# The MLP norm's weights: from per-partition factors after the turn to a row that is multiplied in with the token scale

## The chip, the cores and the metric

One Trainium2 chip, one of its cores. The time is device microseconds of one execution of the whole kernel; that of a kernel is the median of its runs. Engines are called as in the profile: PE (matrix products and transposes; PEld loads their weights), DVE (vector engine), ACT (scalar engine), POOL (here it issues DMAs), SP (issues most of the weight loads).

## The reference, cut to what matters

One layer of a decoder: 2048 prompt tokens and 64 sample tokens, 1024 channels, float32.

```
x = x + W_out [ RMSNorm(attention) || RMSNorm(o * h_mlstm) ]
x = x + channel_mlp(x, norm_mlp, w_up, w_down)

def rmsnorm(x, g):
    y = x * rsqrt(mean(x * x) + EPS)
    return y * g

def channel_mlp(x, g, w_up, w_down):
    h = rmsnorm(x, g)                    # g is norm_mlp, 1024 values
    u = maximum(h @ w_up, 0)
    return (u * u) @ w_down
```

## The kernel before

The tokens are worked off in four quarters of 512 (four tiles of 128; the last quarter has a fifth tile of 64 sample tokens). Each quarter goes through the input projection, attention and the mLSTM, the output projection, the norm that this change is about, and the MLP. Float32 products are made of two halves: each operand is split into a high part (rounded to fp32r by a Copy on ACT) and a low part (the difference, on DVE), and three matmuls are added. So the MLP's input is wanted as `a_hi` and `a_lo`, with channels on the partitions, and also whole in `x_all` (`x_flat`), since from the third unit on the up projection is done in seven products of half size, whose operands are sums of parts of `x_all` (`x_sums` on DVE, `t_high_part` on ACT, `t_low_part` on DVE).

Every engine's order of work is written out by hand; semaphores (`Signal`) tie them. Around the norm, in a quarter that is not the last:

- ACT: `square_tile` of tiles 0 and 1 (sum of squares L886, root L888), `high_tile(0)` (L897), the high part of the first half of the first up weights (`split_act`, L838), `high_tile(1)`, the second half, `square_tile` 2 and 3, `high_tile` 2 and 3, then the high parts of the next unit's weights, then the T parts of the sums and `plain_up` (L1243: Relu of the first up products).
- DVE: for each tile five short instructions for the token scale and `norm_tile` (L1518: x times the token scale, 128x1024); reads of the output projection (`op_at`); for each tile `take_tile` (the turned tile in PSUM times the weights, into `x_all`) and `low_tile` (`a_lo`); between them `split_vec` (L1417: low parts of the weights). Both `take_tile` and `low_tile` show as L1456, the helper for every tensor_tensor. The order is: norm 0, two reads, norm 1, take 0, low 0, read, weights, take 1, low 1, weights, two reads, norm 2, norm 3, take 2, low 2, take 3, low 3, two weights, `x_sums`.
- PE: `turn` (L2511: eight transposes of one tile into two PSUM banks of 4 to 7) of tiles 0 and 1 between the last products of the output projection (L2470 to L2472); then it waits for the low parts of the first up weights and of tiles 0 and 1, does the first up products on these two tiles, with `turn` of tiles 2 and 3 in between, waits for the low parts of all tiles (`nlow`), does the other half, the next up unit (L2470 to L2472), and then the seven products (L2987 to L2989). A bank of `turn` may be written again when `xf_ok` says that its `x_all` part is done.
- POOL: small DMAs. In each quarter it copies eight rows for the mLSTM (`lines`), and after the last product of the MLP's up projection loads the bias tables of the attention again (`bias_again`), since their memory, `bias`, is shared with the MLP's buffers. `sc_read` counts the attention's reads of the bias tables (L1890).

In the last quarter there are five tiles, in the order 0, 1, sample, 2, 3, and ACT does the square of the third tile between `high_tile(0)` and `high_tile(1)`, and both halves of the first up weights after `high_tile(1)`.

The weights `norm_mix`, `norm_attn_out`, `norm_mlstm_out` and `norm_mlp` are read at the start as 24 rows of 128 and turned once (`gains_turn`), so that each channel's weight is a value of its partition.

Of the kernel before, what the change touches and what calls it, by code (L numbers as in the profile page):

```python
# [6 lines left out]
F32 = mybir.dt.float32  # L7
F32R = mybir.dt.float32r
I32 = mybir.dt.int32
ALU = mybir.AluOpType  # L10
ACT = mybir.ActivationFunctionType
# [3 lines left out]
P = 128  # L15
D = 1024
KT = D // P
SEQ = 2048
DECB, DECT = 8, 8
NS = DECB * DECT  # L20
H, KVH, DH = 8, 2, 64
# [16 lines left out]
BLK = TQ // P  # L38
# [145 lines left out]
def norm_order(NT):  # L184

    return [0, 1, BLK, 2, 3] if NT > BLK else [0, 1, 2, 3]
# [22 lines left out]
def hymba_layer(nc, x_prompt, x_sample, cache_k_win, cache_v_win, state_C, state_n, state_m, rel_bias,  # L209
# [5 lines left out]
    with ctx:  # L215
        def sb(name, shape, dt=F32, where=ctx):
            return where.enter_context(nc.sbuf_tensor(name, shape, dt))
# [12 lines left out]
        a_hi = sb("a_hi", [P, KT, TMAX], F32R)  # L230
        a_lo = sb("a_lo", [P, KT, TMAX + NS], F32R)
        sample_parts, sample_again = slice(TQ, TMAX + NS), slice(TMAX, TMAX + NS)
        x1_forms = other("x1_forms", [P, BLK + 1, D], F32R)
        x1 = sb("x1", [P, BLK + 1, D])
        square = sb("square", [P, 4, P])
        ident, triu, ntriu, cmask = (square[:, i, :] for i in range(4))
        kwin = other("kwin", [P, P], F32)[:, 0:KVH * DH]
        ones = sb("ones", [P, P], F32R)
        gains = sb("gains", [P, 3, KT])
        g_final = sb("g_final", [P, D])  # L240
        nsink = sb("nsink", [P, H])
        sink = sb("sink", [P, H])
# [7 lines left out]
        PT = sb("PT", [P, 4, 4 * P])  # L250
        st = sb("st", [P, 240])
# [28 lines left out]
        bias = sb("bias", [P, H, 2 * P], where=phase)  # L280
# [39 lines left out]
        ps = [ctx.enter_context(nc.psum_tensor(f"ps{b}", [P, 512], F32)) for b in range(8)]  # L320
# [10 lines left out]
        early_vec = signal("early_vec", 0)  # L331
# [5 lines left out]
        xf_ok, t_sum, t_high, t_split = signal("xf_ok", 2 * BLK), signal("t_sum", 4), signal("t_high", 4), signal("t_split", 4)  # L337
# [10 lines left out]
        gains_in = signal("gains_in", 0)  # L348
# [5 lines left out]
        normed = signal("normed", BLK)  # L354
        turned = signal("turned", 2 * BLK)
# [3 lines left out]
        nhigh, nlow = signal("nhigh", 2 * BLK), signal("nlow", 2 * BLK)  # L359
# [16 lines left out]
        sc_out, sc_read = signal("sc_out", 2 * BLK), signal("sc_read", H * BLK)  # L376
# [25 lines left out]
        early_pe = signal("early_pe", 0)  # L402
# [2 lines left out]
        act = signal("act", PER_ACT)  # L405


        gain_rows = PT[0:3 * KT, 0, 0:P]
        bucket = bias[0:NBUCKET + 1, 0:2, :].rearrange("p a b -> p (a b)")[:, 0:3 * P]
        bias_by_distance = bias[0:H, 2:4, :].rearrange("p a b -> p (a b)")[:, 0:3 * P]  # L410
        rel_rows = bias[0:NBUCKET + 1, 4, 0:H]
# [6 lines left out]
        def xn_tile(j):  # L418
            return wide[:, 4 * (j % 2):4 * (j % 2) + 4, :].rearrange("p a b -> p (a b)")
# [103 lines left out]
        def x_flat(last):  # L523

            w = TMAX + NS if last else TMAX
            starts = (4 * w, 8 * w + (2 * TQ if last else 4 * TMAX))
            return [x_all[:, at:at + 4 * v].rearrange("p (k t) -> p k t", k=4) for at, v in zip(starts, (w, TMAX))]
# [27 lines left out]
        def spare():  # L555

            return t_plain[:, 0:D]

        def turned_bank(q, n):

            return n % 4
# [135 lines left out]

        @block.gpsimd
        def _(pool):
            for row, g in ((0, norm_mix), (8, norm_attn_out), (12, norm_mlstm_out), (16, norm_mlp)):  # L700
                src = g[0, :].rearrange("(k p) -> k p", p=P)
                pool.dma_start(gain_rows[row:row + src.shape[0], :], src).then_inc(gains_in.sem, 16)
            pool.wait_ge(x_in[3].sem, x_in[3].at(0, 16))
# [23 lines left out]
            def lines(q):  # L727

                if q:
                    pool.wait_ge(m_out.sem, m_out.at(q, 0))  # L730
                pool.wait_ge(r_rows.sem, r_rows.at(q, 2))
                for j in range(BLK):
                    for n, part in enumerate((Mhigh, Mlow)):
                        pool.dma_start(Mline[32 * j + n:32 * j + n + 1, :].rearrange("p (h t) -> p h t", h=HM), part[:, j, :]).then_inc(m_line.sem, 16)

            for q in range(QM):
                lines(q)
# [10 lines left out]
            with nc.allow_non_contiguous_dma("n, and short rows of the bias"):  # L748
                for h in range(H):
                    g, par = h // GQ, h % 2  # L750
# [62 lines left out]
        def _(eng):  # L813
# [76 lines left out]
            def high_tile(q, NT, k):  # L890

                n = norm_order(NT)[k]
                R = NS if n == BLK else P
                s = slice(n * P, n * P + R)
                for m in range(2):
                    eng.wait_ge(xf_ok.sem, xf_ok.at(q, 2 * k + m + 1))
                    eng.activation(a_hi[:, 4 * m:4 * m + 4, s], x_flat(NT > BLK)[m][:, :, s], ACT.Copy).then_inc(nhigh.sem, 1)  # L897

            def high_heads(q, j):

# [508 lines left out]
        def _(eng):  # L1409
# [45 lines left out]
            def tt(out, a, b, op):  # L1455
                return eng.tensor_tensor(out, a, b, op)  # L1456
# [54 lines left out]
            def norm_tile(q, NT, k):  # L1511

                n = norm_order(NT)[k]
                R = NS if n == BLK else P
                scale_tile(q, n, k + 1, root_count(NT > BLK, k))
                if k >= 2:
                    eng.wait_ge(turned.sem, turned.at(q, 2 * (k - 1)))
                eng.tensor_scalar(xn_tile(k)[0:R, :], x1[0:R, n, :], st[0:R, 132 + n:133 + n], None, ALU.mult).then_inc(normed.sem, 1)  # L1518

            def take_tile(q, NT, k):  # L1520

                n = norm_order(NT)[k]
                R = NS if n == BLK else P
                for m in range(2):
                    eng.wait_ge(turned.sem, turned.at(q, 2 * k + m + 1))
                    gain = gains[:, 2, 4 * m:4 * m + 4].unsqueeze(2).broadcast_to([P, 4, R])
                    tt(x_flat(NT > BLK)[m][:, :, n * P:n * P + R], ps[4 + (2 * k + m) % 4][:, 0:4 * R].rearrange("p (k t) -> p k t", k=4), gain, ALU.mult).then_inc(xf_ok.sem, 1)

            def low_tile(q, NT, k):

                n = norm_order(NT)[k]
                R = NS if n == BLK else P
                s = slice(n * P, n * P + R)
                for m in range(2):
                    eng.wait_ge(nhigh.sem, nhigh.at(q, 2 * k + m + 1))
                    tt(a_lo[:, 4 * m:4 * m + 4, s], x_flat(NT > BLK)[m][:, :, s], a_hi[:, 4 * m:4 * m + 4, s].bitcast(F32), ALU.subtract).then_inc(nlow.sem, 1)

            def final_norm(q):

# [451 lines left out]
            def quarter(q, last):  # L1991
# [220 lines left out]
                if last:  # L2212
                    op_at(3, BLK)
                    norm_tile(q, NT, 1)
                    take_tile(q, NT, 0)
                    low_tile(q, NT, 0)
                    op_at(2, 2)
                    norm_tile(q, NT, 2)
                    take_tile(q, NT, 1)
                    low_tile(q, NT, 1)  # L2220
                    op_at(2, 3)
                    split_vec(eng, q, U_M, 0)
                    op_at(3, 2)
                    split_vec(eng, q, U_M, 1)
                    take_tile(q, NT, 2)
                    low_tile(q, NT, 2)
                else:
                    op_at(2, 2)
                    norm_tile(q, NT, 1)
                    take_tile(q, NT, 0)  # L2230
                    low_tile(q, NT, 0)
                    op_at(2, 3)
                    split_vec(eng, q, U_M, 0)
                    take_tile(q, NT, 1)
                    low_tile(q, NT, 1)
                    split_vec(eng, q, U_M, 1)
                    op_at(3, 2)
                op_at(3, 3)
                norm_tile(q, NT, NT - 2)
                norm_tile(q, NT, NT - 1)  # L2240
                take_tile(q, NT, NT - 2)
                low_tile(q, NT, NT - 2)
                take_tile(q, NT, NT - 1)
                low_tile(q, NT, NT - 1)
                ws, c_at, s1, r6, h5, s5 = staging(last)

                def x_sums():

                    one, two = x_flat(last)
                    x11, x12, x21, x22 = one[:, :, HT:TQ], one[:, :, 0:HT], two[:, :, HT:TQ], two[:, :, 0:HT]  # L2250
                    eng.wait_ge(nlow.sem, nlow.at(q, 2 * NT))
                    tt(x11, x12, x11, ALU.subtract).then_inc(t_sum.sem, 1)
                    tt(x12, x22, x12, ALU.subtract).then_inc(t_sum.sem, 1)
                    eng.wait_ge(t_sum.sem, t_sum.at(q, 2))
                    tt(x22, x22, x11, ALU.subtract).then_inc(t_sum.sem, 1)
                    if last:
                        tt(two[:, :, TQ:TMAX], two[:, :, TQ:TMAX], one[:, :, TQ:TMAX], ALU.subtract)
                    eng.wait_ge(t_sum.sem, t_sum.at(q, 3))
                    tt(x21, x22, x21, ALU.subtract).then_inc(t_sum.sem, 1)
# [177 lines left out]
            root_ahead(0, 0)  # L2437
            first_scale(0)
            eng.wait_ge(early_pe.sem, early_pe.at(0, 1))
            eng.tensor_copy(gains[:, :, :].rearrange("p a k -> p (a k)"), ps[7][:, 0:3 * KT]).then_inc(early_vec.sem, 1)  # L2440
            split_vec(eng, 0, 0, 0)
            eng.wait_ge(early_vec.sem, early_vec.at(0, 1))
            for m in range(4):
# [17 lines left out]
        def _(eng):  # L2461
# [63 lines left out]

            def gains_turn():

                eng.wait_ge(gains_in.sem, gains_in.at(0, 16 * 4))
                eng.transpose(ps[7][:, 0:3 * KT], gain_rows, ident[0:3 * KT, 0:3 * KT]).then_inc(early_pe.sem, 1)

            def first_turn(b):

# [599 lines left out]
```

## Time and profile before

| | us |
|---|---|
| median of 3 runs | 2346.86 (2346.73 to 2352.06) |
| the profiled execution | 2347.0 |
| its span on the core | 2345.2 |
| PE busy in the span | 2300.8 |
| DVE, ACT, POOL busy | 1665.1, 1104.1, 94.6 |

The profiled execution's time is the span and 1.8 us around it. The granted clock of PE was 0.997 of full speed in the mean. The busy times of a matmul overlap with the next one's, so PE's idle time is read from the waits and the timeline.

### The profile page before, as it was taken

Reading aid. Unit: us, or ns where it says so; the run is one execution under the profiler, and the core shown is the slowest. Engines: PE = TensorE matmul, PEld = TensorE weight load, DVE = VectorE, ACT = ScalarE, POOL = GpSimd, SP = SyncE. Lnnn points to the kernel's source line nnn. Section 1 sums busy time; section 2 is a strip of 40 time slices with the busy share of each in tenths; the row PEclk is TensorE's granted clock in tenths of the full one; section 3 lists DMA queues with packets and bytes.
Section 4 is the critical chain, followed back from the end, with each engine's and each line's share of the span. In section 5 each row is a group of like instructions: output and inputs, shape, how many; then the busy total and the mean of one; then the engine's idle time right before and its main releaser. Section 6 shows DMA issues by size and latency. Waiting matters only on the chain.

```text
span 2345.2 us, 37363 instructions
## 1 busy us (share of the span) xinstructions
PE 2300.8 (98%) x14430; PEld 2040.1 (87%) x14430; DVE 1665.1 (71%) x3597; ACT 1104.1 (47%) x2110; POOL 94.6 (4%) x161
## 2 busy tenths in 40 slices
PE   9999999999999999999999999999999999999998
PEld 8987899888897898898998788999878878989986
DVE  4478877777368877777456887777755788776775
ACT  4445544445345644455333554444534545444433
POOL 3000000000000000000000220000110000000000
PEclk9999999999999999999999999999999999999999
DMA  6212333234511232334521232333444112222222
GB/s 196 81 46 80 99 99 102 96 100 152 167 56 54 73 100 95 103 99 144 159 81 37 62 94 96 108 99 101 160 123 135 43 53 82 91 90 82 90 81 77
DMA packets 176652, 227.93 MB, mean 97 GB/s; under 512 B 15507, under 2 KB 126708, under 8 KB 176460
## 3 DMA queue, kind: packets, MB, share of 16 engines
q1 hardware_dynamic: 162636, 192.63, 26.4%
q10 hardware_dynamic: 6448, 19.40, 2.3%
q0 software_dynamic: 7392, 13.52, 2.0%
q8 instruction: 115, 1.88, 0.3%
q14 instruction: 61, 0.50, 0.1%
HBM read 214.13 MB, written 12.60 MB: 97 GB/s over the span
## 4 chain that ended last, share of the span: by engine, by line
PE 88%; DVE 8%; ACT 2%; issue 1%; DVEq 0%; ACTq 0%
PE ps L2470 18%; PE ps L2472 18%; PE ps L2471 18%; PE ps L2987 8%; PE ps L2988 8%; PE ps L2989 8%; PE ps L2481 2%; PE ps L2615 2%; PE ps L2595 1%; DVE w_lo L1417 1%; DVE a_lo L1456 1%; PE ps L2604 1%; PE ps L2661 1%; PE ps L2664 1%; DVE x_all L1456 1%
## 5 line engine op out<-in xcount | busy, mean ns | idle before, releaser
L2470 PE MATMUL ps<-w_hi,u_all 128*128 128x512 f32 x1024 | 403.1, 394 | 1.4 <-DVE w_lo L1417 1.4
L2472 PE MATMUL ps<-w_hi,u_all 128*128 128x512 f32 x1024 | 404.2, 395 | 0.0
L2471 PE MATMUL ps<-w_lo,u_all 128*128 128x512 f32 x1024 | 400.2, 391 | 0.0
L1456 DVE TENSOR_TENSOR x<-x,ps 128x512 f32<-128x512 f32 (+1 forms) x288 | 196.3, 684 | 135.1 <-PE ps L2472 117.4
L866 ACT ACTIVATE w_hi<-PT 128x512 fp32r<-128x512 f32 x224 | 128.4, 621 | 340.4 <-PE ps L2472 237.1
L2470 PE MATMUL ps<-w_hi,a_hi 128*128 128x290 f32 (+1 forms) x768 | 262.0, 341 | 1.3 <-DVE x L1456 0.9
L2987 PE MATMUL ps<-a_hi,w_hi 128*128 128x256 f32 (+1 forms) x896 | 255.5, 285 | 1.4 <-DVE wide L1456 1.4
L2988 PE MATMUL ps<-a_lo,w_hi 128*128 128x256 f32 (+1 forms) x896 | 255.8, 285 | 0.0
L2989 PE MATMUL ps<-a_hi,w_lo 128*128 128x256 f32 (+1 forms) x896 | 255.2, 285 | 0.0
L2471 PE MATMUL ps<-w_lo,a_hi 128*128 128x290 f32 (+1 forms) x768 | 252.6, 329 | 0.0
L2472 PE MATMUL ps<-w_hi,a_lo 128*128 128x290 f32 (+1 forms) x768 | 252.4, 329 | 0.0
L2472 PEld LDWEIGHTS ps<-w_hi,u_all 128*128 128x128 f32 x1024 | 192.1, 188 | 44.3
L2471 PEld LDWEIGHTS ps<-w_lo,u_all 128*128 128x128 f32 x1024 | 192.4, 188 | 43.0
L2470 PEld LDWEIGHTS ps<-w_hi,u_all 128*128 128x128 f32 x1024 | 192.3, 188 | 43.0 <-DVE w_lo L1417 2.7
L1456 DVE TENSOR_TENSOR wide<-ps,wide 128x256 f32<-128x256 f32 (+2 forms) x350 | 140.0, 415 | 112.8 <-PE ps L2989 110.9
L1417 DVE TENSOR_TENSOR w_lo<-w_raw,w_hi 128x1024 fp32r<-128x1024 f32 (+1 forms) x160 | 176.5, 1114 | 52.8 <-ACT w_hi L838 52.8
L2470 PE MATMUL ps<-a_hi,w_hi 128*128 128x512 f32 (+2 forms) x552 | 188.7, 342 | 12.2 <-DVE a_lo L1456 8.0
L1223 ACT ACTIVATE wide<-wide 128x512 f32<-128x512 f32 (+1 forms) x112 | 72.3, 645 | 254.7 <-DVE wide L1456 254.7
L2472 PE MATMUL ps<-a_hi,w_lo 128*128 128x512 f32 (+2 forms) x552 | 187.2, 339 | 0.0
L2471 PE MATMUL ps<-a_lo,w_hi 128*128 128x512 f32 (+2 forms) x552 | 186.9, 339 | 0.0
L2987 PEld LDWEIGHTS ps<-a_hi,w_hi 128*128 128x128 f32 x896 | 169.1, 189 | 4.4 <-DVE wide L1456 2.0
L2988 PEld LDWEIGHTS ps<-a_lo,w_hi 128*128 128x128 f32 x896 | 169.1, 189 | 2.4
(427 smaller groups left out, 4904.8 us busy)
## 6 DMA issues: line engine op xcount, KB each, us to landing
w_raw<-in_w_up_dram SPq DMA_DIRECT2D x128, 512.0 KB, 4.0
w_raw<-in_w_down_dram SPq DMA_DIRECT2D x128, 512.0 KB, 3.5
w_raw<-in_w_out_dram SPq DMA_DIRECT2D x32, 512.0 KB, 3.5
w_raw<-in_w_in_dram SPq DMA_DIRECT2D x24, 580.0 KB, 4.7
w_raw<-in_w_in_dram SPq DMA_DIRECT2D x22, 512.0 KB, 3.8
w_raw<-in_w_in_dram SPq DMA_DIRECT2D x32, 256.0 KB, 3.0
x<-in_x_prompt_dram ACTq DMA_DIRECT2D x9, 512.0 KB, 5.9
bias<-bias_rows POOLq DMA_DIRECT2D x32, 128.0 KB, 3.5
```

The lines of the kernel that those rows point to most:

```text
L866: eng.activation(form_at(w_hi_all, u, f), form_src(q, u, name), ACT.Copy).then_inc(f_high.sem, 1)
L1223: eng.activation(c_at[phi], c_at[phi], ACT.Relu).then_inc(u_rel.sem, 1)
L1417: ins = eng.tensor_tensor(w_lo_all[:, to:to + b - a], src[:, a:b], w_hi_all[:, to:to + b - a].bitcast(F32), ALU.subtract)
L1456: return eng.tensor_tensor(out, a, b, op)
L2470: eng.matmul(out, lh, rh, start=(k == ks[0]), stop=False)
L2471: eng.matmul(out, lh, rl, start=False, stop=False)
L2472: ins = eng.matmul(out, ll, rh, start=False, stop=(k == last))
L2481: ins = eng.matmul(out, lhs(k), right, start=(k == ks[0] and part == 0), stop=(k == ks[-1] and part == 1))
L2615: ins = eng.matmul(values_at(g)[:, h, :], PT[:, 2 * g + half, h * P:(h + 1) * P], vv[:, j + half, g, :], start=(half == 0), stop=(half == 1))
L2987: eng.matmul(out, hi[:, k, :], rh, start=(k == 0), stop=False)
L2988: eng.matmul(out, hi[:, k, :], rl, start=False, stop=False)
L2989: ins = eng.matmul(out, lo[:, k, :], rh, start=False, stop=(k == 3))
```

## The change

The weights of the MLP norm are no longer turned: they are read, in each quarter, as one row of 1024 values copied to all 128 partitions (512 KB), by a DMA of POOL, into the first half of the bias tables' memory (`g_mlp`), once the quarter's last score has been read. `norm_tile` multiplies by the token scale and this row in one `scalar_tensor_tensor`. `take_tile` is gone. ACT makes `a_hi` straight from the turned tile in PSUM, DVE makes `a_lo` from the same PSUM bank, and ACT then copies the tile from PSUM to `x_all`, after the low part of that half tile is done. `x_sums` waits for these copies.

```diff
-        gains = sb("gains", [P, 3, KT])
+        gains = sb("gains", [P, 2, KT])
...
-        gain_rows = PT[0:3 * KT, 0, 0:P]
+        gain_rows = PT[0:2 * KT, 0, 0:P]
+        g_mlp = bias[:, 0:4, :].rearrange("p a b -> p (a b)")
...
+        def turned_tile(k, m, R):
+            return ps[4 + (2 * k + m) % 4][:, 0:4 * R].rearrange("p (k t) -> p k t", k=4)
...
-            for row, g in ((0, norm_mix), (8, norm_attn_out), (12, norm_mlstm_out), (16, norm_mlp)):
+            for row, g in ((0, norm_mix), (8, norm_attn_out), (12, norm_mlstm_out)):
...
                         pool.dma_start(Mline[...], part[:, j, :]).then_inc(m_line.sem, 16)
+                pool.wait_ge(sc_read.sem, sc_read.at(q, H * BLK))
+                pool.dma_start(g_mlp, norm_mlp[0, :].partition_broadcast(P)).then_inc(gains_in.sem, 16)
...
             def high_tile(q, NT, k):
                 for m in range(2):
-                    eng.wait_ge(xf_ok.sem, xf_ok.at(q, 2 * k + m + 1))
-                    eng.activation(a_hi[:, 4 * m:4 * m + 4, s], x_flat(NT > BLK)[m][:, :, s], ACT.Copy).then_inc(nhigh.sem, 1)
+                    eng.wait_ge(turned.sem, turned.at(q, 2 * k + m + 1))
+                    eng.activation(a_hi[:, 4 * m:4 * m + 4, s], turned_tile(k, m, R), ACT.Copy).then_inc(nhigh.sem, 1)
+                for m in range(2):
+                    eng.wait_ge(nlow.sem, nlow.at(q, 2 * k + m + 1))
+                    eng.activation(x_flat(NT > BLK)[m][:, :, s], turned_tile(k, m, R), ACT.Copy).then_inc(xf_ok.sem, 1)
...
             def norm_tile(q, NT, k):
-                eng.tensor_scalar(xn_tile(k)[0:R, :], x1[0:R, n, :], st[0:R, 132 + n:133 + n], None, ALU.mult).then_inc(normed.sem, 1)
+                if k == 0:
+                    eng.wait_ge(gains_in.sem, gains_in.at(0, 16 * (3 + q + 1)))
+                eng.scalar_tensor_tensor(xn_tile(k)[0:R, :], x1[0:R, n, :], st[0:R, 132 + n:133 + n], g_mlp[0:R, :], ALU.mult, ALU.mult).then_inc(normed.sem, 1)
-            def take_tile(q, NT, k):
-                ...
             def low_tile(q, NT, k):
-                    tt(a_lo[:, 4 * m:4 * m + 4, s], x_flat(NT > BLK)[m][:, :, s], a_hi[...].bitcast(F32), ALU.subtract).then_inc(nlow.sem, 1)
+                    tt(a_lo[:, 4 * m:4 * m + 4, s], turned_tile(k, m, R), a_hi[...].bitcast(F32), ALU.subtract).then_inc(nlow.sem, 1)
...
                 def x_sums():
-                    eng.wait_ge(nlow.sem, nlow.at(q, 2 * NT))
+                    eng.wait_ge(xf_ok.sem, xf_ok.at(q, 2 * NT))
```

All calls of `take_tile` in DVE's order are dropped, and `gains_turn` turns 16 rows after three DMAs.

## Rows read from the trace of the kernel before

**Rows 1.** The page, part 1: busy time and share of the span of each engine.
```profile
PE 2300.8 (98%) x14430; PEld 2040.1 (87%) x14430; DVE 1665.1 (71%) x3597; ACT 1104.1 (47%) x2110; POOL 94.6 (4%) x161
```

**Rows 2.** Waits of PE: in total, times, longest, in us.
```profile
PE ps L2470 <- DVE a_lo L1456: 8.0, 4, 2.0
PE ps L2470 <- DVE w_lo L1417: 5.3, 6, 1.5
```

**Rows 3.** Timeline of PE, first quarter: start, duration, what, idle before and its releaser.
```profile
224.17 0.39 PE L2470 MATMUL ps<-a_hi,w_hi 128*128 128x256 f32 x1 [1.20 <-DVE w_lo L1417]
...
227.92 1.09 PE L2511 MATMUL ps<-square,wide 128*128 128x128 f32 x8 [0.62 <-DVE wide L1518]
...
234.73 0.39 PE L2470 MATMUL ps<-a_hi,w_hi 128*128 128x256 f32 x1 [1.99 <-DVE a_lo L1456]
...
251.68 0.28 PE L2987 MATMUL ps<-a_hi,w_hi 128*128 128x256 f32 x1
...
255.28 0.36 PE L2987 MATMUL ps<-t_all,w_hi 128*128 128x256 f32 x1 [0.58 <-DVE w_lo L1456]
```

**Rows 4.** Timeline of DVE, first quarter (x2: two merged, duration of both).
```profile
214.96 0.75 DVE L1518 TENSOR_SCALAR wide<-x,st 128x1024 f32<-128x1024 f32 x1
...
217.01 1.29 DVE L1456 TENSOR_TENSOR a_lo<-x_all,a_hi 128x512 fp32r<-128x512 f32 x2
...
218.82 1.22 DVE L1417 TENSOR_TENSOR w_lo<-w_raw,w_hi 128x1024 fp32r<-128x1024 f32 x1
...
222.89 1.23 DVE L1417 TENSOR_TENSOR w_lo<-w_raw,w_hi 128x1024 fp32r<-128x1024 f32 x1 [0.26 <-ACT w_hi L838]
...
228.75 0.75 DVE L1518 TENSOR_SCALAR wide<-x,st 128x1024 f32<-128x1024 f32 x1
...
233.39 1.29 DVE L1456 TENSOR_TENSOR a_lo<-x_all,a_hi 128x512 fp32r<-128x512 f32 x2
...
250.20 1.29 DVE L1456 TENSOR_TENSOR w_lo<-w_raw,w_hi 128x512 fp32r<-128x512 f32 x2
```

**Rows 5.** Timeline of ACT, first quarter.
```profile
213.78 0.29 ACT L888 ACTIVATE st<-st 128x1 f32<-128x1 f32 x1
...
217.48 1.05 ACT L838 ACTIVATE w_hi<-w_raw 128x1024 fp32r<-128x1024 f32 x1
...
221.81 1.05 ACT L838 ACTIVATE w_hi<-w_raw 128x1024 fp32r<-128x1024 f32 x1
...
233.86 1.99 ACT L838 ACTIVATE w_hi<-w_raw 128x1024 fp32r<-128x1024 f32 x2
...
251.88 0.60 ACT L1243 ACTIVATE wide<-ps 128x512 f32<-128x512 f32 x1 [1.04 <-PE ps L2472]
```

**Rows 6.** Groups of instructions of DVE: count, busy us, mean ns of one.
```profile
L1456 DVE TENSOR_TENSOR x_all<-ps,gains 128x512 f32<-128x512 f32 (+1 forms) x34 | 21.3, 666 | 0.0
...
L1456 DVE TENSOR_TENSOR a_lo<-ps,a_hi 128x512 fp32r<-128x512 f32 x16 | 11.0, 687 | 5.0 <-ACT a_hi L902 5.0
```

**Rows 7.** Timeline of DVE, then ACT: two pairs done back to back.
```profile
583.05 2.48 DVE L1547 SCALAR_TENSOR_TENSOR wide<-x,st,g_final 128x1024 f32<-128x1024 f32 x2
...
131.77 1.07 ACT L1101 ACTIVATE PT<-ps 128x512 f32<-128x512 f32 x2
```

**Rows 8.** Line 1890, the scores with their bias: count, ns, first and last start.
```profile
L1890 DVE CUSTOM_DVE_ANT_0 wide<-ps,bias x120: 417/420/425, 100.5 to 1843.2; 128x256 f32<-128x256 f32 x120
```

**Rows 9.** DMA issues: queue, count, KB each, us from issue to landing.
```profile
vm<-in_cache_k_win_dram POOLq DMA_DIRECT2D x1, 512.0 KB, 6.9
```

**Rows 10.** Timeline of ACT, last quarter.
```profile
1928.57 1.04 ACT L886 ACTIVATE PT<-x 64x1024 f32<-64x1024 f32 x1
...
1933.40 2.00 ACT L838 ACTIVATE w_hi<-w_raw 128x1024 fp32r<-128x1024 f32 x2
...
1947.81 1.99 ACT L838 ACTIVATE w_hi<-w_raw 128x1024 fp32r<-128x1024 f32 x2
```

**Rows 11.** Timeline of PE, last quarter.
```profile
1956.28 0.36 PE L2470 MATMUL ps<-a_hi,w_hi 128*128 128x256 f32 x1 [0.37 <-ACT wide L1243]
```

More of the change, by code:

```diff
@@ L1517, in norm_tile @@
                     eng.wait_ge(turned.sem, turned.at(q, 2 * (k - 1)))
-                eng.tensor_scalar(xn_tile(k)[0:R, :], x1[0:R, n, :], st[0:R, 132 + n:133 + n], None, ALU.mult).then_inc(normed.sem, 1)
-            def take_tile(q, NT, k):
[L1522 to L1527, printed above, removed]
+                if k == 0:
+                    eng.wait_ge(gains_in.sem, gains_in.at(0, 16 * (3 + q + 1)))
+                eng.scalar_tensor_tensor(xn_tile(k)[0:R, :], x1[0:R, n, :], st[0:R, 132 + n:133 + n], g_mlp[0:R, :], ALU.mult, ALU.mult).then_inc(normed.sem, 1)
             def low_tile(q, NT, k):
@@ L1535, in low_tile @@
                     eng.wait_ge(nhigh.sem, nhigh.at(q, 2 * k + m + 1))
-                    tt(a_lo[:, 4 * m:4 * m + 4, s], x_flat(NT > BLK)[m][:, :, s], a_hi[:, 4 * m:4 * m + 4, s].bitcast(F32), ALU.subtract).then_inc(nlow.sem, 1)
+                    tt(a_lo[:, 4 * m:4 * m + 4, s], turned_tile(k, m, R), a_hi[:, 4 * m:4 * m + 4, s].bitcast(F32), ALU.subtract).then_inc(nlow.sem, 1)
             def final_norm(q):
@@ L2214, in quarter @@
                     norm_tile(q, NT, 1)
-                    take_tile(q, NT, 0)
                     low_tile(q, NT, 0)
@@ L2218, in quarter @@
                     norm_tile(q, NT, 2)
-                    take_tile(q, NT, 1)
                     low_tile(q, NT, 1)
@@ L2224, in quarter @@
                     split_vec(eng, q, U_M, 1)
-                    take_tile(q, NT, 2)
                     low_tile(q, NT, 2)
@@ L2229, in quarter @@
                     norm_tile(q, NT, 1)
-                    take_tile(q, NT, 0)
                     low_tile(q, NT, 0)
@@ L2233, in quarter @@
                     split_vec(eng, q, U_M, 0)
-                    take_tile(q, NT, 1)
                     low_tile(q, NT, 1)
@@ L2240, in quarter @@
                 norm_tile(q, NT, NT - 1)
-                take_tile(q, NT, NT - 2)
                 low_tile(q, NT, NT - 2)
-                take_tile(q, NT, NT - 1)
                 low_tile(q, NT, NT - 1)
@@ L2439, in _ @@
             eng.wait_ge(early_pe.sem, early_pe.at(0, 1))
-            eng.tensor_copy(gains[:, :, :].rearrange("p a k -> p (a k)"), ps[7][:, 0:3 * KT]).then_inc(early_vec.sem, 1)
+            eng.tensor_copy(gains[:, :, :].rearrange("p a k -> p (a k)"), ps[7][:, 0:2 * KT]).then_inc(early_vec.sem, 1)
             split_vec(eng, 0, 0, 0)
@@ L2526, in gains_turn @@
             def gains_turn():
-                eng.wait_ge(gains_in.sem, gains_in.at(0, 16 * 4))
-                eng.transpose(ps[7][:, 0:3 * KT], gain_rows, ident[0:3 * KT, 0:3 * KT]).then_inc(early_pe.sem, 1)
+                eng.wait_ge(gains_in.sem, gains_in.at(0, 16 * 3))
+                eng.transpose(ps[7][:, 0:2 * KT], gain_rows, ident[0:2 * KT, 0:2 * KT]).then_inc(early_pe.sem, 1)
             def first_turn(b):
```

## The prediction

> **What bounds the kernel now.** The page first: PE is busy for 98% of the span, DVE for 71%, ACT for 47% [rows 1]. So time can only come out of PE's few waits, and can only be lost by making new ones. The waits of PE come next [rows 2]: 8.0 us in four waits of 2.0 for `a_lo` and 5.3 us in six for `w_lo` of L1417. The timeline of PE places them: in the first quarter, around the norm, 1.20 us before the first up product (224.17), 0.62 before the transposes of tile 2 (227.92) and 1.99 before the second half of the up products (234.73) [rows 3]. The first row of the fence is a wait for weights, not for a tile: `w_lo` of the second half unit. That matters, because ACT makes the weights' high part between two tiles, and this change gives ACT more to do there. The second and third quarter repeat these waits at the same places. Beyond them comes a 0.58 wait at 255.28, between the second and the third of the seven products [rows 3].
>
> So the question is which of two chains is late afterwards: the tiles' (norm product, transposes, `a_hi`, `a_lo`), which the change shortens by a multiplication, or ACT's written order, in which the next weights now stand behind two copies, each of which waits for DVE.
>
> **The parts and their prices.**
> Removed: `take_tile`, on DVE, two instructions a tile, 0.67 us in the mean [rows 6]; 34 in all, 21.3 us busy.
> Changed: the norm product. A tensor_scalar of 128x1024 takes 0.75 us [rows 4]. The new form is that of L1547: the same tile, a scalar column and a second tile, 2.48 us for two [rows 7], so 1.28 each, with the next instruction 1.20 after the start (two records overlap by some 0.08). That is +0.53 us each, 16 times (and once for the samples), and each stands on the chain.
> Moved: `a_hi` reads PSUM, `a_lo` reads PSUM. `a_lo` from PSUM took 0.687 [rows 6], and from SBUF 1.29 for two [rows 4]: the same, price nothing.
> Added on ACT: two copies of 128x512 from PSUM a tile. L1101 is the same, 1.07 for two [rows 7]: 0.59 each, the next 0.48 after the start.
> The copy waits for `a_lo`, so behind it on ACT wait the weights' high part (or the next tile's `a_hi`), and behind that DVE's `w_lo` and PE. A rule of the Trainium skill bears on this wait (PSUM — Partial Sum Buffer, Terms): two engines that read one bank at once are an error there. By it the copy can't run beside the subtraction; no run here shows it, and no number below hangs on it.
> Another page would move a number: by ScalarE: Activation LUTs, What ACT_TABLE_LOAD costs, a copy is 186 ns and 0.833 ns an element, less 93 ns of overlap, so an estimated 0.52 between starts of 512 elements instead of the 0.48 of [rows 7]; the sum below would be some 0.6 us higher. I take the row.
> Added on POOL: one wait and one DMA of 512 KB a quarter. The wait is for the last score; in the last quarter that is at 1843.2 [rows 8]. A DMA of this size from POOL landed in 6.9 us [rows 9]. The norm's work in that quarter is around 1930 [rows 10], so the row is there some 70 us early: price nothing, at both ends, unless POOL itself came late by that much. The waits behind it on POOL's queue are for events later than the last score. At the start one small DMA and 8 of 24 turned rows fall away: nothing, since PE warms up meanwhile.
>
> **The sum, first quarter.** I replay the written order with these durations; an instruction starts 0.04 after its last releaser, or when its engine is free.
> Tiles 0 and 1: the product of tile 0 moves the read behind it, ACT's square and root of tile 1 (213.78) and the product of tile 1 (214.96) by 0.53, so DVE is free at 216.69. `a_hi` of tile 0 is long there (ACT is free at 214.60, the tile is turned), so the two subtractions run 216.69 to 217.98, before 217.01 to 218.30. ACT's second copy starts at 218.02, and ACT is free at 218.50; the first weights' high part started at 217.48 [rows 5], so +1.02. It ends at 219.55, and `w_lo` starts at 219.59 where it stood at 218.82 [rows 4]: DVE is free at 220.73. Subtractions of tile 1 to 222.02, second copy from 222.06, ACT free at 222.54, second weights +0.73 on 221.81, `w_lo` at 223.63, +0.74 on 222.89. PE's first up product comes at 224.91: +0.74. A wait has grown, though DVE has less to do.
> Tiles 2 and 3: +0.74 and the longer product, +1.27 at the transposes (227.92). The product of tile 3 starts at 230.02 (228.75 before), DVE is free at 231.22, subtractions of tile 2 to 232.51, second copy from 232.55, `a_hi` of tile 3 from 233.03, its subtractions 233.66 to 234.95. Before, they ended at 234.68 [rows 4]: +0.27 at PE's 234.73. Here the two multiplications that are gone nearly pay for what came before.
> After that ACT still has the copies of tile 3: free at 235.47, where the next weights started at 233.86 [rows 5], +1.61. The weights' low parts, `x_sums` and everything that ACT and DVE do up to the first forms is one chain between the two, so DVE's 250.20 moves by 1.61; its first half ends at 252.50, and PE wants it at 251.68 [rows 3]: a new wait, +0.85. Two products later ACT's Relu at 251.88, which had idled 1.04 [rows 5], has taken up most of the shift: about +0.5 at 255.28. So a quarter loses 0.5 us; three lose 1.5.
>
> **The last quarter.** ACT has the third tile's square behind the copies of tile 0 (+0.9 at 1928.57), and the weights behind those of tile 1 (+1.35 at 1933.40) [rows 10]. With the product's 0.53 the fourth tile's transposes are 1.65 late instead of 1.27, and 0.4 more stays to the end: 1.61 and 0.4 are +2.0 at 1947.81. PE there waited 0.37 for ACT's L1243 [rows 11], the end of the same chain, with nothing between: +2.0 in full.
> Sum: 1.5 + 2.0 = +3.5 us. Against the profiled execution's 2347.0 that is 2350.5; the median of the runs is 0.14 lower, so 2350.4.
> The bounds: copies at 0.40 between starts would give an estimated +2, at 0.60 (DVE's price for a tile of this size, [rows 4]) +6. If the product still cost 0.75, its lower end, the sum would be -5.5: the tiles' chain would then win. L1547 has the same operands, so I take 1.28.
>
> **Rivals.** What a measurement tells from no change is about 0.3%, 7 us.
> A, faster: ACT, with half its time free [rows 1], takes the copies in the gaps in which it waits for a tile anyway, so that they don't hold up weights. If a copy cost nothing but its wait, the second copies of tiles 0 to 2 (0.48 each) would be off the path: +0.27 at 234.73 becomes -1.2, and that stays, since the later wait goes too; in the last quarter five such copies take its 2.0 to -0.2. Sum -3.8, 2343. Between this and +3.5 at 0.48 the sign changes at about 0.25 us a copy. If the copies held up nothing at all, PE's three waits of a quarter (1.20, 0.62 and 1.99, [rows 3]) could go, 3.8 us, at most 15 us in four quarters; the replay without copies gives -13.4, 2333.5. Against it: the copies stand ahead of the weights in ACT's order.
> B, slower: the +1.61 after the norm isn't taken up at 251.88 but stays with PE in all quarters (DVE's order from 250.20 on has little air), 3 x 1.61 + 2.0 = 6.8, 2353.8; and if a copy takes 0.75 between starts, because two engines work in the same banks, six copies stand on the path of a quarter and nine on that of the last, 0.27 more each: some +7.2 on the sum, 2357.6.
> C, nothing: each move falls into a wait that PE has anyway (1.99 at 234.73), and the stage ends where it did: 2347.
>
> **How the numbers follow.** My forecast, a small loss between 2348 and 2353: 0.60. A 0.16, of which 0.05 lies within 7 us. B 0.17, beyond 7 us. C 0.07. So same 0.60 + 0.05 + 0.07 = 0.72, faster 0.11, slower 0.17. The range takes in A's near end (2343) and B as far as 2355; it leaves out A's far end and a third to a half of B.
>
> **What the profile afterwards would show.** The norm product at 1.28. PE's wait for `w_lo` of L1417 at the first up product about 0.7 longer a quarter; that for the product of tile 2 about 0.5 longer; that for `a_lo` shorter, about 1.0 instead of 2.0, though the stage's end is 0.3 later. ACT's weights behind the norm 1.6 later against the last transposes, a new wait of some 0.8 before the first of the seven products, and in the last quarter a wait for L1243 of about 1.6. DVE's busy time lower by some 12 us (21.3 less, 9 more), ACT's higher by 20. Wrong would be: weights that don't move, copies that ACT does in 0.25, or a wait of DVE for the row of weights.

## The result and the profile after

The changed kernel takes 2356.66 us (median of 6 runs, 2355.67 to 2357.64), the kernel before 2348.42 beside it (6 runs, 2346.73 to 2352.27): ratio 1.0032, 95% interval 1.0022 to 1.0041. Slower, by 8 us where 3.5 were forecast, and outside the range. The profiled execution takes 2357.64, its span is 2355.8, 10.6 more than before.

The page of the changed kernel, part 1 and the three groups of the MLP's down products (a row names the operand that moves through PE first, here `w_hi` or `w_lo`, 512 columns; then the one that PEld has loaded, here 128x128 of `u_all`):

```profile
PE 2310.4 (98%) x14430; PEld 2042.0 (87%) x14430; DVE 1651.9 (70%) x3563; ACT 1119.8 (48%) x2144; POOL 94.1 (4%) x164
...
L2466 PE MATMUL ps<-w_hi,u_all 128*128 128x512 f32 x1024 | 406.7, 397 | 1.5 <-DVE w_lo L1427 1.5
L2467 PE MATMUL ps<-w_lo,u_all 128*128 128x512 f32 x1024 | 405.2, 396 | 0.0
L2468 PE MATMUL ps<-w_hi,u_all 128*128 128x512 f32 x1024 | 404.3, 395 | 0.0
```

The same groups on the page of the kernel before:

```profile
L2470 PE MATMUL ps<-w_hi,u_all 128*128 128x512 f32 x1024 | 403.1, 394 | 1.4 <-DVE w_lo L1417 1.4
L2472 PE MATMUL ps<-w_hi,u_all 128*128 128x512 f32 x1024 | 404.2, 395 | 0.0
L2471 PE MATMUL ps<-w_lo,u_all 128*128 128x512 f32 x1024 | 400.2, 391 | 0.0
```

This is the first surprise: PE is busy 9.6 us longer [rows 1] with as many instructions as before, and 8.7 of it (1216.2 against 1207.5) lie in three groups that the change doesn't touch and ahead of which there is no new idle time. DVE's busy time is 13.2 lower and ACT's 15.7 higher; some 12 and 20 were forecast.

Waits of PE in the changed kernel, the four that belong to the norm:

```profile
PE ps L2507 <- DVE wide L1530: 7.0, 9, 1.5
PE ps L2466 <- DVE w_lo L1427: 6.7, 7, 1.5
PE ps L2466 <- DVE a_lo L1466: 3.9, 4, 1.0
...
PE ps L2466 <- ACT wide L1253: 1.7, 1, 1.7
```

The first of them, for the norm product, has doubled; before it was:

```profile
PE ps L2511 <- DVE wide L1518: 3.3, 5, 1.0
```

Timeline of PE, first quarter of the changed kernel:

```profile
226.13 0.39 PE L2466 MATMUL ps<-a_hi,w_hi 128*128 128x256 f32 x1 [1.45 <-DVE w_lo L1427]
...
230.41 1.09 PE L2507 MATMUL ps<-square,wide 128*128 128x128 f32 x8 [1.16 <-DVE wide L1530]
...
236.21 0.38 PE L2466 MATMUL ps<-a_hi,w_hi 128*128 128x256 f32 x1 [0.98 <-DVE a_lo L1466]
...
253.87 0.36 PE L2983 MATMUL ps<-a_hi,w_hi 128*128 128x256 f32 x1 [0.56 <-DVE w_lo L1466]
...
256.96 0.36 PE L2983 MATMUL ps<-t_all,w_hi 128*128 128x256 f32 x1
```

Timelines of ACT and of DVE at the same place:

```profile
218.63 1.20 ACT L907 ACTIVATE x_all<-ps 128x512 f32<-128x512 f32 x2 [1.82 <-DVE a_lo L1466]
219.72 1.05 ACT L845 ACTIVATE w_hi<-w_raw 128x1024 fp32r<-128x1024 f32 x1
...
236.68 2.00 ACT L845 ACTIVATE w_hi<-w_raw 128x1024 fp32r<-128x1024 f32 x2
```

```profile
216.71 1.28 DVE L1530 SCALAR_TENSOR_TENSOR wide<-x,st,bias 128x1024 f32<-128x1024 f32 x1
```

Everything in this execution stands 1.28 us late before the norm begins (an ACT row at 141.21 before is at 142.49); a later execution of the same kernel has that row at 141.23, so the 1.28 belong to the execution. Taken off, the norm stage is almost the one forecast:

| | before | after | shift less 1.28 | forecast |
|---|---|---|---|---|
| first up product, PE [rows 3] | 224.17 | 226.13 | +0.68 | +0.74 |
| transposes of tile 2, PE [rows 3] | 227.92 | 230.41 | +1.21 | +1.27 |
| second half of the up products [rows 3] | 234.73 | 236.21 | +0.20 | +0.27 |
| next weights, ACT [rows 5] | 233.86 | 236.68 | +1.54 | +1.61 |
| first of the seven products [rows 3] | 251.68 | 253.87 | +0.91 | +0.85 |
| third of the seven products [rows 3] | 255.28 | 256.96 | +0.40 | +0.5 |

The second quarter loses 0.4 as the first does (entered 3.4 late, the third of its seven products 3.87). The third loses only 0.1 (6.1 and 6.21): PE had stood longer for the weights there before the change already, as the two rows show, before and after.

```profile
1350.47 0.39 PE L2470 MATMUL ps<-a_hi,w_hi 128*128 128x256 f32 x1 [1.47 <-DVE w_lo L1417]
```

```profile
1356.95 0.39 PE L2466 MATMUL ps<-a_hi,w_hi 128*128 128x256 f32 x1 [1.44 <-DVE w_lo L1427]
```

In the last quarter PE's product behind L1253 comes 8.50 late [rows 11]:

```profile
1964.78 0.36 PE L2466 MATMUL ps<-a_hi,w_hi 128*128 128x256 f32 x1 [1.71 <-ACT wide L1253]
```

The stage was entered 6.4 late, so the quarter loses 2.1 (forecast 2.0). The norm stages are 3.1 of the 10.6.

The rest comes between two norm stages. Two rows of ACT, ten periods of the MLP apart (one down unit and one set of seven products each), in the kernel before and then in the changed one:

```profile
303.58 0.63 ACT L1223 ACTIVATE wide<-wide 128x512 f32<-128x512 f32 x1 [4.09 <-DVE wide L1456]
...
514.18 0.63 ACT L1223 ACTIVATE wide<-wide 128x512 f32<-128x512 f32 x1 [4.09 <-DVE wide L1456]
```

```profile
305.41 0.63 ACT L1233 ACTIVATE wide<-wide 128x512 f32<-128x512 f32 x1 [4.11 <-DVE wide L1466]
...
517.35 0.63 ACT L1233 ACTIVATE wide<-wide 128x512 f32<-128x512 f32 x1 [4.11 <-DVE wide L1466]
```

Ten periods take 210.60 us before and 211.94 after: 0.13 a period, no wait, just a slower step. From the third of a quarter's seven products to the start of the next quarter the shift grows by 1.8, 2.2, 1.6 and (to the end) 2.1 us, 7.7 in all. What is left, -1.5, is clock. The granted clock, by 20 us (columns: stretch, length, PE busy and its instructions, clock, DMA share, GB/s), of the kernel before and of the changed one:

```profile
1740.00:1760.00 20.00, 20.00 (x146) 0.83 0.22 52
```

```profile
1740.00:1760.00 20.00, 19.94 (x167) 0.91 0.35 87
```

Each is one stretch at half clock (1.2 GHz) outside the norm stages, some 6.8 us long before and 3.5 after. So 1.3 + 3.1 + 7.7 - 1.5 = 10.6.

What could slow the down products? The diff has one line that reaches them: `gains` shrinks from 96 to 64 bytes a partition, and the tensors are laid one behind another, so each tensor behind `gains` moves down by 32 bytes. In the built programs `u_all` begins at byte 166688 of a partition before and at 166656 after; `w_hi` and `w_lo`, which lie ahead of `gains`, stay. Modulo 128, `u_all` goes from 32 to 0, the weights stay at 96. The theory to test: the place. The rivals: the new order of ACT and DVE, the row's DMA, or chance.

### The profile page after: what moved, and what is told of

Its sections match the earlier page's. It is cut to its first block, busy times and chain, and to the rows that moved or that the text cites. A ratio compares the mean times of both kernels' runs of the same rounds, so it can differ in the third digit from the quotient of the medians.

```text
span 2355.8 us, 37370 instructions
## 1 busy us (share of the span) xinstructions
PE 2310.4 (98%) x14430; PEld 2042.0 (87%) x14430; DVE 1651.9 (70%) x3563; ACT 1119.8 (48%) x2144; POOL 94.1 (4%) x164
## 4 chain that ended last, share of the span: by engine, by line
PE 86%; DVE 8%; ACT 3%; issue 2%; DMA 0%; DVEq 0%; ACTq 0%
PE ps L2466 18%; PE ps L2467 17%; PE ps L2468 17%; PE ps L2984 8%; PE ps L2983 8%; PE ps L2985 8%; PE ps L2477 2%; PE ps L2611 2%; DVE w_lo L1427 1%; PE ps L2591 1%; PE ps L2600 1%; DVE wide L1530 1%; PE ps L2657 1%; ACT w_hi L845 1%; PE ps L2660 1%
## 5 line engine op out<-in xcount | busy, mean ns | idle before, releaser
L2467 PE MATMUL ps<-w_lo,u_all 128*128 128x512 f32 x1024 | 405.2, 396 | 0.0
```

What stands on the lines that cost most here:

```text
L2467: eng.matmul(out, lh, rl, start=False, stop=False)
```

## The experiments

Times are medians; the kernel before was timed again beside each group of runs (2348.9 to 2349.5).

### e1: the changed kernel with its tensors put back

```diff
-        gains = sb("gains", [P, 2, KT])
+        gains = sb("gains", [P, 3, KT])
-            eng.tensor_copy(gains[:, :, :]..., ps[7][:, 0:2 * KT])
+            eng.tensor_copy(gains[:, 0:2, :]..., ps[7][:, 0:2 * KT])
```

> The changed kernel with the small tensor of gains as large as before (96 instead of 64 bytes a partition), so that every tensor behind it lies where it lay before; no instruction differs. If the drift in the down units comes from where the tensors lie (theory: 32 bytes), the step from the second to the third matmul of a down group goes back from 0.235 to 0.227 us, PE's busy time from 2310 to about 2301, and the time is +3 to +4 us over the kernel before, ratio 1.0015. If it comes from the new order of ACT and DVE or from the row's DMA, nothing changes: about +8 us, ratio 1.0032 to 1.0035.

2347.78 us (11 runs), ratio 1.0001, interval 0.9992 to 1.0010. The busy times of the page's groups are those of before to the last digit:

```profile
L2466 PE MATMUL ps<-w_hi,u_all 128*128 128x512 f32 x1024 | 403.1, 394 | 1.3 <-DVE w_lo L1427 1.3
L2468 PE MATMUL ps<-w_hi,u_all 128*128 128x512 f32 x1024 | 404.2, 395 | 0.0
L2467 PE MATMUL ps<-w_lo,u_all 128*128 128x512 f32 x1024 | 400.2, 391 | 0.0
```

So the 8.9 us between the changed kernel and e1 hung on 32 bytes that nothing uses. But the time is not 3 to 4 us over the kernel before, as this theory had it; see the clock, below.

### e2 and e7: the kernel before with its tensors moved

e2, 32 bytes behind `gains`; e7, the last block of tensors alone 32 bytes down.

```diff
+        pad = sb("pad", [P, KT])                  # e2, behind gains
...
-        sinkc = sb("sinkc", [P, 4])               # e7
-        nsinkc = sb("nsinkc", [P, 4])
+        sinks = sb("sinks", [P, 8])
+        sinkc, nsinkc = sinks[:, 0:4], sinks[:, 4:8]
```

> The kernel before with 32 unused bytes a partition behind the gains, which gives all later tensors the phase within 64 bytes that they have after the change; no instruction differs. Place theory: the down units drift as after the change, PE busy about 2310, and the time is +5 to +7 us, ratio 1.002 to 1.003, with not one of the change's instructions in it. Theory of the new order or of the row's DMA: no difference, ratio 1.000.

> The kernel before with the same joining: u_all at byte 166656, no instruction of the change in it. Theory of u_all's place: the down units drift here too, +6 to +9 us over the kernel before, ratio 1.003 to 1.004, PE busy 2308 to 2312. If the drift needs the change's new order of ACT and DVE as well: no difference, ratio 1.000.

e2: 2350.79, ratio 1.0006 (0.9998 to 1.0015), groups 395, 392, 394 ns: the theory in its first form (32 bytes modulo 64) falls. e7: 2354.75, ratio 1.0027 (1.0017 to 1.0036), with the changed kernel's pace and none of its instructions; the ratio stays a little under the expected 1.003. Its row:

```profile
L2471 PE MATMUL ps<-w_lo,u_all 128*128 128x512 f32 x1024 | 405.3, 396 | 0.0
```

### e3, e6, e5: which tensor, and chance

e3 is the changed kernel with 32 unused bytes ahead of the last block alone; e6 is e1 with the joining of e7, so that the last block alone is moved; e5 is the changed kernel again.

> The changed kernel with the 32 bytes put ahead of the last block of tensors alone (u_all, t_all, x_all and what lies over them), so that these lie as before and those between the gains and them (wide, PT, st, g_final, kk, vv) as after. If it is the place of the moving operand u_all that slows the down products, as e1: +3 to +4 us, ratio 1.0015, step 0.227. If it is the place of wide, PT or st, no change against the changed kernel: +8 us, step 0.235.

> The changed kernel with gains as large as before, and two 16-byte columns joined into one tensor of 32 bytes, so that the last block alone (u_all, t_all, x_all and what lies over them) begins 32 bytes earlier, at byte 166656 of a partition, where the change had put it; all else lies as before. Theory of u_all's place: drift as in the changed kernel, +8 to +9 us over e1, about 2356, PE busy 2310. If it was the place of the tensors between the gains and the block, together with the block's: as e1, 2348.

> The changed kernel as it is, beside the three others of this call on one chip. If its slow down units belong to the kernel, 2355 to 2358 us, PE busy about 2310, mean of the second matmul of a down group 396 ns. If they belonged to the chip or the hour of its first measurement (theory: chance), it is where its twin with the tensors put back was: 2347 to 2349, busy 2300.

e3: 2349.11, ratio 1.0001 (0.9992 to 1.0010), 394, 391, 395 ns: the pace of e1, and as there without the 3 to 4 us over the kernel before. e6: 2355.19, ratio 1.0024 (1.0015 to 1.0034), 397, 396, 395 ns. e5: 2356.3, ratio 1.0030 (1.0018 to 1.0041), 397, 396, 395 ns. So it is neither chance nor the tensors between (e6 stays 1.1 under e5, which no run explains); of the last block, the down products read `u_all` only. It is the operand that is loaded: the expectation of e3 calls it the moving one, the wrong way round. End to end the place is worth 8.9 us between the changed kernel and e1, 7.4 between e6 and e1, and 5.4 between e7 and the kernel before; the three groups' busy time grows by 9.0 in e6 and e7 and by 8.7 in the changed kernel, and the medians scatter with the clock (below).

### e8, e10, e13: its own place, or its distance from the weights

```diff
+        pad = sb("pad", [P, 32])                  # e8, ahead of the last block
...
+        pad0 = sb("pad0", [P, 8])                 # e10 and e13, ahead of w_hi
+        pad1 = sb("pad1", [P, 24])                # e10 also, ahead of the last block
```

> The changed kernel with 128 unused bytes ahead of the last block: u_all at byte 166784, a multiple of 128 as 166656 is, but not of 256. The kernel before shifted by 32 had u_all at 166720, a multiple of 64 alone, and its down groups kept their pace (395, 392 and 394 ns). If multiples of 128 are slow: as the changed kernel, 2356, busy 2310. If only multiples of 256 are, or this one place alone: as e1 and e3, 2348, busy 2300.

> The changed kernel with 32 unused bytes ahead of w_hi and 96 ahead of the last block: u_all at 166784, a multiple of 128 as in the changed kernel and in e8, but w_hi and w_lo now 0 past a multiple of 128, where they stood 96 past one in all runs so far. If u_all's own place sets the pace: slow as e8, 2356 to 2358, PE busy 2309, groups of 397, 397 and 395 ns. If the distance between the weights' and u_all's places sets it: another pace, as fast as e1 (394, 391 and 395 ns, 2348) or slower still.

> The changed kernel with 32 unused bytes ahead of w_hi and nothing else: u_all comes back to byte 166688, 32 past a multiple of 128, its place in the kernel before and in e1, and the weights move to 0 past one, so that u_all lies 32 past the weights again, as in the changed kernel (0 and 96). If the distance modulo 128 sets the pace: slow groups (397, 396 and 395 ns), PE busy 2309, 2355 to 2358 us. If u_all's own place does, with something else behind e10: the pace of e1 (394, 391 and 395 ns), 2348.

e8: 2357.5 (ratio 1.0034). e10: 2341.14, ratio 0.9968 (0.9955 to 0.9981): `u_all` at the same byte as in e8, the weights moved, and 16 us less. e13: 2357.32, ratio 1.0032 (1.0021 to 1.0043): `u_all` where it lies before, and slow. Its own place is not it; the distance is. (With the weights the tensors between them and `gains` move too; the down products read none of these.) A row of e10, which is faster than the kernel before:

```profile
L2469 PE MATMUL ps<-w_lo,u_all 128*128 128x512 f32 x1024 | 397.7, 388 | 0.0
```

### e14: the best distance in the kernel before

64 unused bytes (`pad = sb("pad", [P, 16])`) ahead of the last block.

> The kernel before with 64 unused bytes ahead of the last block: u_all 96 past a multiple of 128, as the weights are, distance 0. If the distance sets the pace, with or without the change's instructions: groups of 394, 391 and 388 ns as in e10, 6.5 us off the kernel before's 2349, about 2342.5, in single runs 2338 to 2346 by the clock. If e10 and e11 were fast for something in the change: no difference, ratio 1.000.

2342.4, ratio 0.9965 (0.9952 to 0.9977). All kernels by distance (`u_all` less weights, modulo 128 bytes; ns in the order high·high, low·high, high·low of weights and `u_all`; busy us of the three groups):

| distance | kernels | weights, `u_all` | ns | busy |
|---|---|---|---|---|
| 0 | e10; e11, e14 | 0, 0; 96, 96 | 394, 388, 391; 393, 389, 391 | 1201.6; 1201.9 |
| 32 | changed, e5 to e8; e13 | 96, 0; 0, 32 | 397, 396, 395 (e8: 397, 395, 397) | 1216.1 to 1216.5 |
| 64 | before, e1, e3, e4, e9, e12 | 96, 32 | 394, 391, 395 | 1207.5 |
| 96 | e2 | 96, 64 | 395, 392, 394 | 1209.6 |

### e4: the copies behind what they held up

e1, and on ACT each tile's copies stand later: those of tile 0 behind `a_hi` of tile 1, those of tile 1 behind the second half of the weights, those of tiles 2 and 3 behind `a_hi` of tile 3; in the last quarter, whose lines are left out here, they move in the same way.

```diff
                     split_act(eng, q, last, U_M, 0)
                     high_tile(q, NT, 1)
+                    copy_tile(q, NT, 0)
                     split_act(eng, q, last, U_M, 1)
+                    copy_tile(q, NT, 1)
...
                 high_tile(q, NT, NT - 2)
                 high_tile(q, NT, NT - 1)
+                copy_tile(q, NT, NT - 2)
+                copy_tile(q, NT, NT - 1)
```

> e1, and on ACT the two copies of a tile stand behind the next high parts of weights or tiles instead of ahead of them (the tiles' and weights' high parts keep their order). The replay with the prediction's durations: first up product 1.1 us earlier than in the kernel before, the second half of the up products 3.5 earlier, 2.7 left at the third of the seven products. So some -2.7 a quarter and about as much in the last, -11 us against the kernel before, 2337, ratio 0.9955, if the place theory holds; about 2343 if the drift stays. If the copies hold up nothing where they stand now (rival: the product's longer time alone makes the loss), it equals e1.

2337.95, ratio 0.9955 (0.9942 to 0.9967): 9.8 less than e1. That meets the expected 2337 to a microsecond, in part by luck. In the traces, against the kernel before, the first three quarters gain 2.7, 2.7 and 3.0 us as expected. The last, which was to gain about as much, loses 0.8: PE waits 2.20 there, and 3.4 us at half clock follow. In return the half clock that the kernel before has at 1740 is not there, which gives 2.9.

```profile
1945.40 0.35 PE L2480 MATMUL ps<-a_hi,w_hi 128*128 128x256 f32 x1 [2.20 <-ACT wide L1267]
```

Its timeline of ACT: the weights no longer wait for DVE, and four copies in a row take 1.91 to the next start, 0.48 each.

```profile
217.86 1.06 ACT L845 ACTIVATE w_hi<-w_raw 128x1024 fp32r<-128x1024 f32 x1 [1.08 <-PE ps L2482]
218.82 1.07 ACT L904 ACTIVATE a_hi<-ps 128x512 fp32r<-128x512 f32 x2
219.78 1.09 ACT L913 ACTIVATE x_all<-ps 128x512 f32<-128x512 f32 x2
...
231.58 2.08 ACT L913 ACTIVATE x_all<-ps 128x512 f32<-128x512 f32 x4
233.49 2.05 ACT L845 ACTIVATE w_hi<-w_raw 128x1024 fp32r<-128x1024 f32 x2
```

Its waits of PE, against e1: those for `w_lo` of the weights and for the norm product shrink from 6.5 and 7.0 to 1.3 and 2.0, that for `a_lo` from 3.9 to 0.2, and that ahead of the seven products grows from 1.7 to 3.1.

```profile
PE ps L2997 <- DVE w_lo L1480: 3.1, 3, 1.0
...
PE ps L2480 <- ACT wide L1267: 2.2, 1, 2.2
...
PE ps L2521 <- DVE wide L1544: 2.0, 5, 0.9
```

### e9 and e12: the price of the product, and of a copy

```diff
-                eng.scalar_tensor_tensor(xn_tile(k)..., g_mlp[0:R, :], ALU.mult, ALU.mult)   # e9
+                eng.tensor_scalar(xn_tile(k)..., None, ALU.mult)
...
-                    eng.activation(x_flat(...)[m][:, :, s], turned_tile(k, m, R), ACT.Copy).then_inc(xf_ok.sem, 1)   # e12
+                    for i in range(4):
+                        ins = eng.activation(x_flat(...)[m][:, i, s], turned_tile(k, m, R)[:, i, :], ACT.Copy)
+                    ins.then_inc(xf_ok.sem, 1)
```

> e1 with the norm product as a multiplication by the token scale alone (0.75 instead of 1.28 us; it leaves the norm's weights out, so the output differs). The replay puts the third of the seven products 1.65 us earlier than in the kernel before (e1: 0.47 later) and the end of the last quarter 0.5 earlier (e1: 2.1 later), in sum -5.5 against +3.5: 8.9 us less than e1's 2347.8, so 2339. If the copies alone make the loss (rival), hardly less than e1: 2346 to 2348.

> e1 with each copy as four of 128x128, each some 0.26 to 0.29 us, so 1.0 to 1.1 between the starts of two copies instead of 0.48 (the result is the same). The replay gives +3.9 us a quarter at the third of the seven products and +6.1 in the last quarter, in sum +18 where e1 has +3.5: 14 us over e1, 2362. If ACT took the copies in its gaps (rival A of the prediction), the extra half microsecond would be hidden: 2348 to 2350.

e9, which leaves the norm's weights out: 2338.97, ratio 0.9958 (0.9943 to 0.9973), 8.8 under e1 where 8.9 were expected. The product's half microsecond, 17 times, is worth that much since it stands on every tile's chain. Its waits of PE, all three of the norm lower:

```profile
PE ps L2466 <- DVE w_lo L1427: 4.6, 7, 1.1
PE ps L2507 <- DVE wide L1530: 3.2, 5, 1.0
...
PE ps L2466 <- DVE a_lo L1466: 1.8, 4, 0.5
```

e12: 2354.86 (2351.58 to 2357.57), ratio 1.0023 (1.0013 to 1.0032), 7 over e1 where 14 were expected. The expectation's price was wrong: a pair of copies, now eight instructions, takes 1.27 to the next start (218.35 to 219.62 on ACT's timeline) instead of 1.09, not 2.1.

```profile
218.35 1.47 ACT L908 ACTIVATE x_all<-ps 128x128 f32<-128x128 f32 x8 [1.83 <-DVE a_lo L1468]
219.62 1.12 ACT L845 ACTIVATE w_hi<-w_raw 128x1024 fp32r<-128x1024 f32 x1
```

PE's waits in and behind the norm grow by 1.9 against e1's profile; about 6 more of busy time go with half clock in three stretches (780 to 800, 1340 to 1360, 1740 to 1760). So e12 doesn't weigh the copies well: the extra work was small, and clock came on top.

### e11: a version that beats both

e4 with 64 unused bytes ahead of the last block: distance 0.

> e4 with 64 unused bytes ahead of the last block: u_all 96 past a multiple of 128 (32 past one in e4, 64 in e2, 0 in the slow kernels). If only multiples of 128 are slow: as e4, 2337 to 2338.5, groups of 394, 391 and 395 ns. If the pace differs at each of the four places: some other time, within 10 us of e4.

2331.27, ratio 0.9924 (0.9909 to 0.9939), 6.7 less than e4. That is the change as written, with its copies in other places and 96 bytes of padding (the old size of `gains` and these 64): 18 us under the kernel before instead of 8 over it.

## Why the prediction was wrong, and where it was right

**The step that failed** is the end of the paragraph on POOL and the start: "one small DMA and 8 of 24 turned rows fall away: nothing, since PE warms up meanwhile". That is true of the DMA and of the transposes (the row at 141.21 before is at 141.23 in e5). But the rows also shrink a tensor, and nothing in the sum asked what lies behind it: it moved `u_all` against the weights, and the down products slowed. This term is 7.7 us in the trace and 8.9 between the medians of the changed kernel and e1, more than twice the whole forecast. The norm has no part in it: e7, with the old norm, has the same slow groups. A second term put at nothing, the clock, hid some of it: the measured +8.2 is 8.9 from the place and 3.1 from the norm stages, less some 3.8; this remainder goes with the clock, as far as the counts below show.

**The norm's own sum was nearly right in the trace.** Product 1.28 forecast, 1285 ns in the mean of 16; a copy 0.48 between starts, 0.48 in e4; the shifts as in the table; +0.5 in each of three quarters forecast, 0.4, 0.4 and 0.1 found; the last quarter 2.0 and 2.1. The new wait before the seven products is there, 0.56 of the 0.8. One sign failed: the wait for `w_lo` at the first up product was to grow by 0.7 and grew by 0.25 (1.20 to 1.45). PE itself comes there 0.4 later, since the transposes of tile 1 now wait for their norm product too (0.25 at 218.05), which the replay left out. The 0.52 for a copy by the Trainium skill (ScalarE: Activation LUTs, What ACT_TABLE_LOAD costs) was the worse guess. No run let ACT and DVE read one PSUM bank at once, so the rule of the Trainium skill on that (PSUM — Partial Sum Buffer, Terms) stays untested here.

**But in the median that sum doesn't show.** e1's quarters lose the same 3.1 us in its trace, and its median ties with the kernel before. The kernel before spreads by its clock: in the 27 runs beside e1 to e4 its two extremes are 2344.19 at a mean granted clock of 0.999 and 2352.72 at 0.995, and the times between go down the same line; nine of e1's eleven runs are at 0.998 and within 2347.2 to 2347.9. The profile of e2 (the old norm stage) shows one place where the clock goes. First the wait, in PE's timeline, then the clock around it:

```profile
235.52 0.38 PE L2471 MATMUL ps<-a_hi,w_hi 128*128 128x256 f32 x1 [1.97 <-DVE a_lo L1457]
```

```profile
230.00:234.00 4.00, 3.55 (x31) 1.00 0.00 0
234.00:235.50 1.50, 0.00 (x0) 1.00 0.00 0
235.50:239.00 3.50, 3.48 (x17) 0.54 0.23 49
```

Right after the wait of 1.97, the third within 12 us, the clock is at half for 3.5 us, some 1.7 us lost. e2's four norm stages all have it. Over the four profiles with the old norm stage (before, e2, e7, e14) it is in 7 of 16 stages; over the nine with the new one as the change has it (changed, e1, e3, e5, e6, e8, e10, e13, and e9 with shorter waits still) in none of 36, the longest wait there being 1.5 (and 1.7 behind the last one). The three kernels with other waits fit. e12, with a wait of 1.94 or 1.95 in its first three quarters and of 2.0 in the last, has it in two of four stages; e4 and e11, with one of 2.20 in the last quarter alone, have it in one of four (that quarter) and in none.

```profile
781.82 0.39 PE L2468 MATMUL ps<-a_hi,w_hi 128*128 128x256 f32 x1 [1.95 <-DVE w_lo L1429]
```

So the change gives back in clock about what it loses in order: in place of a wait of 2.0 it has three of 1.0 to 1.5. In sum the waits of the first quarter's stage are 3.8 us before and after. That the shorter longest wait is the reason is inferred from these counts; no run changed that wait alone. The prediction took the profiled execution's time, in which no norm stage had lost clock, and left the clock out. By the Trainium skill (TensorE: Matmul & The Clock Gate, Part 1) the clock gate passes either half of the clock's pulses or all, never a share between; read in steps of half a microsecond, these stretches agree, 0.50 inside and other values only where a stretch begins or ends.

**The rivals.** A (ACT takes the copies in its gaps) is refuted for the order as written: put behind the weights, the copies make e4 9.8 us faster. A's far end, 2333.5, with copies that hold up nothing, is what that other order comes near to. B's end (slower, 2353.8 to 2357.6) holds the measured time by luck, since another mechanism made it: ACT's 1.54 was taken up to 0.40 by the third product, and a copy took 0.48, not 0.75. C is out: the stage's shift is not 0, and that e1's time equals the kernel before's, as C would have it, is the clock's doing. POOL's row was never waited for: ahead of the product on DVE there are 0.6 us of idle time for all sixteen together.

## What to carry to other kernels

A change that resizes one small tensor moves all behind it: compare the built addresses of the operands of the longest loop before pricing anything else, and give the changed kernel a twin with padding, so that the order's effect and the place's are measured apart. Where an engine's order is written by hand, a copy that waits for another engine goes behind whatever doesn't need it; that was worth 9.8 us, some three times what the change's norm stages lost. And where single runs scatter, set them against their granted clock before reading a median.

## What the runs showed that was not expected

The pace of back-to-back 128x512 products depends on how far the loaded operand (`u_all`) lies from the moving one (the weights) modulo 128 bytes of a partition. In steps of 32 bytes, a group of 3072 products is busy for 1201.6 to 1201.9, 1216.1 to 1216.5, 1207.5 or 1209.6 us at distance 0, 32, 64 or 96; 0 and 32 were run at two places of the weights each, 64 and 96 at one, and finer steps not at all. End to end that is up to 16 us of 2350 (e8 and e10), 14.9 of it in these three groups. It shows as no wait: the idle column of the second and third group stays at 0.0, only the mean of a matmul changes, by up to 8 ns. The seven products, whose `t_all` moved along (there `t_all` moves and the weights are loaded), keep their busy times within 1 us a group. Why the distance matters is open, and whether `w_hi` or `w_lo` sets it: in all runs both lay at one place modulo 128. The loads of `u_all` stayed at 187 to 189 ns each.
